# First FFN of a two-block transformer kernel: high and low activations side by side in the up projection, and the gate's row steps in the down stage

## The chip, the cores and the metric

The kernel runs on one core of a Trainium2 chip. The metric is the device time of one execution in microseconds; the time before is the median of three runs, 758.73 us (757.24 to 759.23).

## The reference, cut to what matters

Two transformer blocks on one sequence of 256 rows of width 1024, in fp32. The change touches only the feed-forward part of the first block and the gate `g2`, which is a row vector of 1024:

```python
c_act = jax.nn.silu(c)
mod = c_act @ w_ada[l] + b_ada[l]
sh1, sc1, g1, sh2, sc2, g2 = [m[:, None, :] for m in jnp.split(mod, 6, axis=-1)]
...
h = rmsnorm(x, norm_gains[l, 2]) * (1.0 + sc2) + sh2
y = jnp.square(jax.nn.relu(h @ w1[l] + b1[l])) @ w2[l] + b2[l]
x = x + g2 * rmsnorm(y, norm_gains[l, 3])
```

`w1` is 1024 x 4096, `w2` 4096 x 1024. The second block has a mixer of four branches and a second FFN (SwiGLU, hidden width 2816).

## The kernel before, in words

**Split products.** Every large product is made of three products of fp32r parts: high weight x high activation, high x low, low x high. Weights come in units of 128 x 1024 values (512 KB). Each unit goes through four engines: SyncE (queue SP) loads it into one of four slots of `raw`; ScalarE (ACT) rounds it to its high part `wh` (`round_unit`, L614); VectorE (DVE) subtracts that from `raw` to get the low part `wl` (`low_unit`, L1000); TensorE (PE) multiplies. The rings `raw`, `wh`, `wl` have four slots each. ACT may round unit u when PE has finished unit u - 4 (semaphore `unit_done`), DVE follows (`rounded`), PE starts unit u when DVE is through (`split_ready`), and SP loads unit u + 4 once DVE is through with unit u. ACT and DVE run `AHEAD` = 3 units ahead of PE: while PE is on unit u, they prepare unit u + 3. The order of each engine's work is written out by hand, and every wait is on the engine that stands in the list: what comes behind it waits too.

**Up stage of the first FFN (units `U_UP1` to `U_UP1` + 31).** A loop of eight turns with four units in each (`RING` = 4). Unit k gives 128 hidden columns for all 256 rows, in PSUM bank `acc[k % 4]`. The transposed activations `xT` hold the high parts in columns 0 to 255 and the low parts in 256 to 511. PE does `col_unit` (L1445 to L1447): for each of 8 k-tiles three matmuls of 256 columns, all into the same 256 columns of the bank. For each unit, ACT rounds the weights of unit k + 3, makes relu with bias out of the bank (L803, which frees the bank), and squares it into the high part of `hid` (L805). DVE makes the low weights of unit k + 3 (L1000), the exact square (L1202) and the low part of `hid` (L1205).

**The gate's rows.** `g2` is summed as rows: for each of 8 row blocks of `w_ada` (128 x 1024, 512 KB) ACT's queue issues a load into `xr[:, 0, :]` (`rows_tmp`, L808), and DVE adds block x c to `G2` (L1210, 128 x 1024). There is one buffer: a load waits for the step before it (`g2_used`), a step waits for its load (`g2_full`). In the kernel before, one such load and one such step stand in each of the eight turns of the up loop. After the eighth, GpSimd multiplies `G2` by the gain (L570). PE sums it over the partitions after 28 of the 32 down units.

**Down stage (units `U_DOWN1` to `U_DOWN1` + 31).** `wide_unit`: 12 matmuls of 512 columns for a unit, into all four banks (L1466 to L1468). Beside it ACT only rounds (`round_down1`) and DVE only makes low weights (`low_down1`), except for the bias `b2`: behind its first turn of four units ACT clears and rounds `b2parts` (L823, L824, three times L811); behind the third and the fifth turn it rounds two rows and one row more. DVE subtracts for it behind its second turn (two instructions of L1214) and behind its fourth (one).

**The second FFN's up stage** runs much later (570 to 697 us) and uses `both_unit` (L1458, L1459): for each k-tile one matmul of 512 columns (high weight x high and low activations side by side) and one of 256 (low weight x high). ACT copies the right half of the bank (L978), DVE adds the left half to it (L1412).

Of the kernel before, what the change touches and what calls it, by code (L numbers as in the profile page):

```python
# [50 lines left out]
RING = 4  # L51
# [15 lines left out]
V_B1, V_CONV, V_GQ, V_GK, V_BSP, V_ROWS = 16, 48, 54, 55, 56, 60  # L67
# [110 lines left out]
def build_program(nc, a):  # L178
# [25 lines left out]
    with ctx:  # L204
# [3 lines left out]
        def sem(name):  # L208
            return ctx.enter_context(nc.semaphore(name))
# [142 lines left out]
        arg_psum, w_exped, w_masked, pvs_done, sb_ready, fox_ready = (sem(n) for n in ("arg_psum", "w_exped", "w_masked", "pvs_done", "sb_ready", "fox_ready"))  # L352
        dve_step, pool_step = sem("dve_step"), sem("pool_step")
        out_ready, out_done = sem("out_ready"), sem("out_done")
        b2_zeroed, b2_high, b2_rest = sem("b2_zeroed"), sem("b2_high"), sem("b2_rest")
        f_parts = sem("f_parts")
        wf_zeroed = sem("wf_zeroed")
# [3 lines left out]
        def slot_of(u):  # L361
            return u % RING
# [243 lines left out]
        def _(act):  # L606
# [15 lines left out]
            def round_looped(u0, i, k):  # L622

                s, count = raw_place(u0 + k)
                round_unit(raw_full[s], raw_slot(s), 16 * count + 16 * i, u0 + k - RING + 1 + RING * i, s)
# [169 lines left out]
                high_columns(X_UP1, r)  # L795
            round_static(U_UP1 + 2)

            with act.Fori(0, D_FF // P // RING) as i:
                for k in range(RING):
                    round_looped(U_UP1 + AHEAD, i, k)  # L800
                    act.wait_ge(unit_done, U_UP1 + k + 1 + RING * i)
                    act.wait_ge(hid_ready, RING * i + k + 1)
                    A(act_t[:, k, :], acc[k][:, 0:ROWS], ACT.Relu, bias=vT[:, bass.ds(V_B1 + k + RING * i, 1)]).then_inc(acc_free, 1)  # L803
                    act.wait_ge(acc_free, F_PROJ1 + k + 1 + RING * i)
                    A(hid[:, RING * i + k, 0:ROWS], act_t[:, k, :], ACT.Square).then_inc(hid_hi, 1)  # L805
                    if k == 1:
                        act.wait_ge(g2_used, i + 1)
                        act.dma_start(xr[:, 0, :], w_ada_rows[bass.ds(P * i, P), D * C_G2:]).then_inc(g2_full, 16)  # L808
            def b2_round(row):

                A(b2parts[row:row + 1, :], b2row[row:row + 1, :], ACT.Copy).then_inc(b2_high, 1)  # L811

            def round_down1(first, count):

                with act.Fori(0, count) as i:
                    for k in range(RING):
                        round_looped(U_DOWN1 + AHEAD + RING * first, i, k)

            round_down1(0, 1)
            act.wait_ge(late_loaded, 16 * 8)  # L820
            act.wait_ge(unit_done, U_DOWN1)
            for half in range(2):
# [2 lines left out]
            act.wait_ge(b2_zeroed, 2)  # L825
            for row in (0, 32, 64):
                b2_round(row)
            round_down1(1, 2)
            act.wait_ge(b2_rest, 2)
            for row in (32, 64):  # L830
                b2_round(row)
            round_down1(3, 2)
            act.wait_ge(b2_rest, 3)
            b2_round(64)
            round_down1(5, D_FF // P // RING - 6)
# [151 lines left out]
        def _(dve):  # L987
# [207 lines left out]
            low_static(U_UP1 + 1)  # L1195
            low_static(U_UP1 + 2)

            with dve.Fori(0, D_FF // P // RING) as i:
                for k in range(RING):
                    low_unit(U_UP1 + AHEAD + k + 1 + RING * i, slot_of(U_UP1 + AHEAD + k), slot_of(U_UP1 + AHEAD + k))  # L1200
                    dve.wait_ge(acc_free, F_PROJ1 + k + 1 + RING * i)
                    V.tensor_tensor(val_t[:, k, :], act_t[:, k, :], act_t[:, k, :], ALU.mult).then_inc(hid_sq, 1)  # L1202
                    dve.wait_ge(hid_sq, RING * i + k + 1)
                    dve.wait_ge(hid_hi, RING * i + k + 1)
                    V.tensor_tensor(hid[:, RING * i + k, ROWS:], val_t[:, k, :], hid[:, RING * i + k, 0:ROWS].bitcast(f32),  # L1205
                                    ALU.subtract).then_inc(hid_ready, 1)

                dve.wait_ge(g2_full, 16 * i + 32)
                dve.wait_ge(g2_used, i + 1)
                V.scalar_tensor_tensor(out=G2[:, :], in0=xr[:, 0, :], scalar=cT[:, bass.ds(i, 1)], in1=G2[:, :],  # L1210
                                       op0=ALU.mult, op1=ALU.add).then_inc(g2_used, 1)
            def b2_remainder(row):

                V.tensor_tensor(b2row[row:row + 1, :], b2row[row:row + 1, :], b2parts[row:row + 1, :].bitcast(f32), ALU.subtract).then_inc(b2_rest, 1)  # L1214

            def low_down1(first, count):

                with dve.Fori(0, count) as i:
                    for k in range(RING):
                        u = U_DOWN1 + AHEAD + RING * first + k  # L1220
                        low_unit(u + 1 + RING * i, slot_of(u), slot_of(u))

            low_down1(0, 2)
            dve.wait_ge(b2_high, 3)
            for row in (32, 64):
                b2_remainder(row)
            low_down1(2, 2)
            dve.wait_ge(b2_high, 5)
            b2_remainder(64)
            low_down1(4, D_FF // P // RING - 5)  # L1230
# [199 lines left out]
        def _(pe):  # L1430
# [5 lines left out]
            def col_unit(u, wait, bank, moving, waits=None):  # L1436

                s = slot_of(u)
                pe.wait_ge(split_ready, wait)
                for kt in range(KT):  # L1440
                    if waits is not None:
                        pe.wait_ge(xT_ready, waits(kt))
                    w = slice(P * kt, P * (kt + 1))
                    hi, lo = moving[:, kt, 0:ROWS], moving[:, kt, ROWS:]
                    mm(bank[:, 0:ROWS], wh[:, s, w], hi, start=(kt == 0), stop=False)  # L1445
                    mm(bank[:, 0:ROWS], wh[:, s, w], lo, start=False, stop=False)  # L1446
                    ins = mm(bank[:, 0:ROWS], wl[:, s, w], hi, start=False, stop=(kt == KT - 1))  # L1447
                ins.then_inc(unit_done, 1)

            def both_unit(u, wait, bank, moving, waits=None):  # L1450

                s = slot_of(u)
                pe.wait_ge(split_ready, wait)
                for kt in range(KT):
                    if waits is not None:
                        pe.wait_ge(xT_ready, waits(kt))
                    w = slice(P * kt, P * (kt + 1))
                    mm(bank[:, :], wh[:, s, w], moving[:, kt, :], start=(kt == 0), stop=False, skip_group_check=True)  # L1458
                    ins = mm(bank[:, 0:ROWS], wl[:, s, w], moving[:, kt, 0:ROWS], start=False, stop=(kt == KT - 1),  # L1459
                             skip_group_check=True)  # L1460
                ins.then_inc(unit_done, 1)
# [83 lines left out]
            def columns_ready(t):  # L1545

                return lambda kt: X_COUNT * t + KT + 2 * (kt // 2) + 2
# [169 lines left out]
            with pe.Fori(0, D_FF // P // RING) as i:  # L1717
                for k in range(RING):
                    pe.wait_ge(acc_free, F_PROJ1 - RING + k + 1 + RING * i)
                    col_unit(U_UP1 + k, U_UP1 + k + 1 + RING * i, acc[k], xT, columns_ready(X_UP1) if k == 0 else None)  # L1720
            n_hid = D_FF // P
            for k in range(n_hid - RING):
                pe.wait_ge(hid_ready, RING + k + 1)
# [222 lines left out]
```

## Time and profile before

| | |
|---|---|
| median of three runs | 758.73 us (757.24 to 759.23) |
| the profiled execution | 759.55 us |
| its span, first to last instruction | 757.8 us |
| PE busy (matmul) | 722.2 us, 95% |
| PE weight loads | 615.5 us, 81% |
| DVE busy | 513.7 us, 68% |
| ACT busy | 444.4 us, 59% |
| GpSimd busy | 37.8 us, 5% |
| DMA | 152.07 MB, mean 201 GB/s |
| granted TensorE clock | 1.000 |

The profile is of one execution. Matmuls are pipelined, so the duration of one (some 0.28 us for 256 columns) is longer than the distance to the next, and only the distances tell the pace. An instruction of DVE can start a little before the end shown for the one in front of it. A wait is shown in brackets behind the instruction that waited, with what released it.

### The profile page before, as it was taken

The numbers are of one execution on the slowest core, as the hardware profiler recorded it, in microseconds if no ns is written. First come the engines' busy times: TensorE is split into PE (matmuls) and PEld (weight loads), VectorE is DVE, ScalarE is ACT, GpSimd is POOL, SyncE is SP. The second block draws the span as 40 slices with busy tenths as digits, with TensorE's granted clock in tenths as the row PEclk, the third lists the DMA queues.
The fourth block names the chain that finished last, engine by engine and source line by source line (L and its number), as shares of the span: only waits on it lengthen the run. The fifth ranks groups of instructions, "written<-read, shape, count | busy, mean of one in ns | idle before, by whom it ended". The sixth has DMA issues, their size and how long they took to land.

```text
span 757.8 us, 12098 instructions
## 1 busy us (share of the span) xinstructions
PE 722.2 (95%) x4126; PEld 615.5 (81%) x4126; DVE 513.7 (68%) x738; ACT 444.4 (59%) x696; POOL 37.8 (5%) x69
## 2 busy tenths in 40 slices
PE   0599999999999999999999999999999999999998
PEld 0488976689999888877989787787788888888886
DVE  6788579788777765447647574856677777777443
ACT  0554768656666654455546497465457777776331
POOL 4000000100000100014102000000000000000000
PEclk9999999999999999999999999999999999999999
DMA  8999778447877766545764654555445665665651
GB/s 309 364 331 378 209 221 301 139 141 220 243 222 255 246 197 195 194 112 136 224 189 146 223 147 134 191 163 180 130 139 167 187 198 171 188 196 194 194 194 56
DMA packets 137554, 152.07 MB, mean 201 GB/s; under 512 B 6189, under 2 KB 111784, under 8 KB 137516
## 3 DMA queue, kind: packets, MB, share of 16 engines
q1 hardware_dynamic: 135714, 146.86, 62.6%
q10 hardware_dynamic: 1804, 4.74, 1.8%
q8 instruction: 22, 0.36, 0.2%
q14 instruction: 14, 0.11, 0.0%
HBM read 150.14 MB, written 1.44 MB: 200 GB/s over the span
## 4 chain that ended last, share of the span: by engine, by line
PE 52%; DVE 2%; issue 0%; ACT 0%; DVEq 0%; ACTq 0%
PE acc L1458 11%; PE acc L1466 10%; PE acc L1467 9%; PE acc L1468 9%; PE acc L1459 6%; PE acc L1447 1%; PE acc L1445 1%; PE acc L1446 1%; PE aux L1434 1%; DVE wl L1000 0%; DVE x_rows L1069 0%; PE aux L1660 0%; ACT wh L614 0%; PE aux L1778 0%; PE aux L1852 0%
## 5 line engine op out<-in xcount | busy, mean ns | idle before, releaser
L1000 DVE TENSOR_TENSOR wl<-raw,wh 128x1024 fp32r<-128x1024 f32 x215 | 263.6, 1232 | 147.0 <-ACT wh L614 146.0
L614 ACT ACTIVATE wh<-raw 128x1024 fp32r<-128x1024 f32 x215 | 226.0, 1056 | 122.4 <-PE acc L1468 116.1
L1445 PE MATMUL acc<-xT,wh 128*128 128x256 f32 x440 | 125.2, 285 | 3.4 <-DVE xT L1042 2.2
L1458 PE MATMUL acc<-xT,wh 128*128 128x512 f32 x352 | 124.5, 399 | 0.3 <-DVE xT L1033 0.3
L1446 PE MATMUL acc<-xT,wh 128*128 128x256 f32 x440 | 124.5, 283 | 0.0
L1447 PE MATMUL acc<-xT,wl 128*128 128x256 f32 x440 | 124.5, 283 | 0.0
L1466 PE MATMUL acc<-wh,xT 128*128 128x512 f32 (+1 forms) x272 | 108.0, 397 | 0.3 <-issue 0.3
L1467 PE MATMUL acc<-wl,xT 128*128 128x512 f32 (+1 forms) x272 | 104.3, 384 | 0.0
L1468 PE MATMUL acc<-wh,xT 128*128 128x512 f32 (+1 forms) x272 | 104.3, 383 | 0.0
L1459 PE MATMUL acc<-xT,wl 128*128 128x256 f32 x352 | 98.9, 281 | 0.0
L1445 PEld LDWEIGHTS acc<-xT,wh 128*128 128x128 f32 x440 | 84.4, 192 | 5.8 <-DVE xT L1042 2.3
L1446 PEld LDWEIGHTS acc<-xT,wh 128*128 128x128 f32 x440 | 84.4, 192 | 0.1
L1447 PEld LDWEIGHTS acc<-xT,wl 128*128 128x128 f32 x440 | 84.4, 192 | 0.0
L1466 PE MATMUL acc<-wh,hid 128*128 128x512 f32 x216 | 84.1, 390 | 0.0
L1467 PE MATMUL acc<-wl,hid 128*128 128x512 f32 x216 | 84.1, 389 | 0.0
L1468 PE MATMUL acc<-wh,hid 128*128 128x512 f32 x216 | 84.0, 389 | 0.0
L1458 PEld LDWEIGHTS acc<-xT,wh 128*128 128x128 f32 x352 | 66.1, 188 | 17.1 <-issue 0.7
L1459 PEld LDWEIGHTS acc<-xT,wl 128*128 128x128 f32 x352 | 66.5, 189 | 0.0
L1466 PEld LDWEIGHTS acc<-wh,xT 128*128 128x128 f32 x272 | 51.1, 188 | 16.2 <-issue 6.6
L1468 PEld LDWEIGHTS acc<-wh,xT 128*128 128x128 f32 x272 | 51.1, 188 | 10.4
L1467 PEld LDWEIGHTS acc<-wl,xT 128*128 128x128 f32 x272 | 51.2, 188 | 9.3 <-issue 0.5
L1466 PEld LDWEIGHTS acc<-wh,hid 128*128 128x128 f32 x216 | 40.6, 188 | 8.4
(278 smaller groups left out, 864.4 us busy)
## 6 DMA issues: line engine op xcount, KB each, us to landing
raw<-in_w_in SPq DMA_DIRECT2D x66, 512.0 KB, 4.1
raw<-in_w SPq DMA_DIRECT2D x64, 512.0 KB, 4.3
raw<-in_w_ffn_in SPq DMA_DIRECT2D x44, 512.0 KB, 4.4
raw<-in_w_ada SPq DMA_DIRECT2D x29, 512.0 KB, 5.9
raw<-in_w_ffn_out SPq DMA_DIRECT2D x22, 512.0 KB, 4.2
raw_more<-in_w_ada SPq DMA_DIRECT2D x11, 512.0 KB, 6.7
raw<-in_w_out SPq DMA_DIRECT2D x11, 512.0 KB, 3.3
rows_tmp<-in_w_ada ACTq DMA_DIRECT2D x8, 512.0 KB
```

The costliest lines, as they stand in the source:

```text
L614: A(wh[:, s, :], raw_unit, ACT.Copy).then_inc(rounded, 1)
L1000: V.tensor_tensor(wl[:, s, :], raw_slot(r), wh[:, s, :].bitcast(f32), ALU.subtract).then_inc(split_ready, 1)
L1434: return mm(out, in_, ident[0:n, 0:n], start=True, stop=True, is_transpose=True)
L1445: mm(bank[:, 0:ROWS], wh[:, s, w], hi, start=(kt == 0), stop=False)
L1446: mm(bank[:, 0:ROWS], wh[:, s, w], lo, start=False, stop=False)
L1447: ins = mm(bank[:, 0:ROWS], wl[:, s, w], hi, start=False, stop=(kt == KT - 1))
L1458: mm(bank[:, :], wh[:, s, w], moving[:, kt, :], start=(kt == 0), stop=False, skip_group_check=True)
L1459: ins = mm(bank[:, 0:ROWS], wl[:, s, w], moving[:, kt, 0:ROWS], start=False, stop=(kt == KT - 1), skip_group_check=True)
L1466: mm(bank, hi, wh[:, s, cols], start=first, stop=False)
L1467: mm(bank, hi, wl[:, s, cols], start=False, stop=False)
L1468: return mm(bank, lo, wh[:, s, cols], start=False, stop=last)
```

## The change

- PE: the up units of the first FFN use `both_unit` instead of `col_unit`. The high activations' product and the low activations' product with the high weights stand side by side in the 512 columns of the bank.
- ACT, up stage: instead of relu with bias, it copies the right half of the bank with the bias added (`up_half`). The high part of `hid` is now a copy of DVE's exact square (`hidden_high`), one unit behind (for the fourth unit of a turn at once).
- DVE, up stage: it adds the left half (`acc_free` comes from here now), makes max(x, 0) * x in one instruction, and makes the low part of `hid` one unit behind (`hidden_low`). The row step is taken out.
- The eight loads and eight row steps of `g2` stand in the down stage: one load ahead of it, the others behind the second and the fourth unit of each turn on ACT, and the steps behind the first and the third unit of each turn on DVE, for the first four turns.
- ACT's wait on `hid_ready` ahead of the relu falls away.

```diff
@@ ACT, up stage
+            def hidden_high(i, k):
+                act.wait_ge(hid_sq, RING * i + k + 1)
+                A(hid[:, RING * i + k, 0:ROWS], val_t[:, k, :], ACT.Copy).then_inc(hid_hi, 1)
+
             with act.Fori(0, D_FF // P // RING) as i:
                 for k in range(RING):
                     round_looped(U_UP1 + AHEAD, i, k)
                     act.wait_ge(unit_done, U_UP1 + k + 1 + RING * i)
-                    act.wait_ge(hid_ready, RING * i + k + 1)
-                    A(act_t[:, k, :], acc[k][:, 0:ROWS], ACT.Relu, bias=vT[:, bass.ds(V_B1 + k + RING * i, 1)]).then_inc(acc_free, 1)
-                    act.wait_ge(acc_free, F_PROJ1 + k + 1 + RING * i)
-                    A(hid[:, RING * i + k, 0:ROWS], act_t[:, k, :], ACT.Square).then_inc(hid_hi, 1)
-                    if k == 1:
-                        act.wait_ge(g2_used, i + 1)
-                        act.dma_start(xr[:, 0, :], w_ada_rows[bass.ds(P * i, P), D * C_G2:]).then_inc(g2_full, 16)
+                    A(act_t[:, k, :], acc[k][:, ROWS:], ACT.Identity, bias=vT[:, bass.ds(V_B1 + k + RING * i, 1)]).then_inc(up_half, 1)
+                    if k >= 1:
+                        hidden_high(i, k - 1)
+                    if k == RING - 1:
+                        hidden_high(i, k)
@@ ACT, down stage
+            def load_gate_rows(first, i):
+                act.wait_ge(g2_used, i + 1 + first)
+                act.dma_start(xr[:, 0, :], w_ada_rows[bass.ds(P * i + P * first, P), D * C_G2:]).then_inc(g2_full, 16)
+
-            def round_down1(first, count):
+            def round_down1(first, count, loads=()):
                 with act.Fori(0, count) as i:
                     for k in range(RING):
                         round_looped(U_DOWN1 + AHEAD + RING * first, i, k)
-            round_down1(0, 1)
+                        if k in loads:
+                            load_gate_rows(2 * first + (k + 1) // 2, 2 * i)
+
+            act.wait_ge(g2_used, 1)
+            act.dma_start(xr[:, 0, :], w_ada_rows[0:P, D * C_G2:]).then_inc(g2_full, 16)
+            round_down1(0, 1, (1, 3))
...
-            round_down1(1, 2)
+            round_down1(1, 2, (1, 3))
...
-            round_down1(3, 2)
+            round_down1(3, 1, (1,))
+            round_down1(4, 1)
@@ DVE, up stage
+            def hidden_low(i, k):
+                dve.wait_ge(hid_hi, RING * i + k + 1)
+                V.tensor_tensor(hid[:, RING * i + k, ROWS:], val_t[:, k, :], hid[:, RING * i + k, 0:ROWS].bitcast(f32),
+                                ALU.subtract).then_inc(hid_ready, 1)
+
             with dve.Fori(0, D_FF // P // RING) as i:
                 for k in range(RING):
                     low_unit(U_UP1 + AHEAD + k + 1 + RING * i, slot_of(U_UP1 + AHEAD + k), slot_of(U_UP1 + AHEAD + k))
+                    dve.wait_ge(up_half, RING * i + k + 1)
+                    V.tensor_tensor(act_t[:, k, :], acc[k][:, 0:ROWS], act_t[:, k, :], ALU.add).then_inc(acc_free, 1)
+                    if k >= 1:
+                        hidden_low(i, k - 1)
                     dve.wait_ge(acc_free, F_PROJ1 + k + 1 + RING * i)
-                    V.tensor_tensor(val_t[:, k, :], act_t[:, k, :], act_t[:, k, :], ALU.mult).then_inc(hid_sq, 1)
-                    dve.wait_ge(hid_sq, RING * i + k + 1)
-                    dve.wait_ge(hid_hi, RING * i + k + 1)
-                    V.tensor_tensor(hid[:, RING * i + k, ROWS:], val_t[:, k, :], hid[:, RING * i + k, 0:ROWS].bitcast(f32),
-                                    ALU.subtract).then_inc(hid_ready, 1)
-
-                dve.wait_ge(g2_full, 16 * i + 32)
-                dve.wait_ge(g2_used, i + 1)
-                V.scalar_tensor_tensor(out=G2[:, :], in0=xr[:, 0, :], scalar=cT[:, bass.ds(i, 1)], in1=G2[:, :],
+                    V.scalar_tensor_tensor(out=val_t[:, k, :], in0=act_t[:, k, :], scalar=0.0, in1=act_t[:, k, :],
+                                           op0=ALU.max, op1=ALU.mult).then_inc(hid_sq, 1)
+                hidden_low(i, RING - 1)
@@ DVE, down stage
+            def gate_rows(first, i):
+                dve.wait_ge(g2_full, 16 * i + 32 + 16 * first)
+                dve.wait_ge(g2_used, i + 1 + first)
+                V.scalar_tensor_tensor(out=G2[:, :], in0=xr[:, 0, :], scalar=cT[:, bass.ds(i + first, 1)], in1=G2[:, :],
                                        op0=ALU.mult, op1=ALU.add).then_inc(g2_used, 1)
-            def low_down1(first, count):
+            def low_down1(first, count, steps_of_two=False):
                 with dve.Fori(0, count) as i:
                     for k in range(RING):
                         u = U_DOWN1 + AHEAD + RING * first + k
                         low_unit(u + 1 + RING * i, slot_of(u), slot_of(u))
-            low_down1(0, 2)
+                        if steps_of_two and k % 2 == 0:
+                            gate_rows(2 * first + k // 2, 2 * i)
+            low_down1(0, 2, True)
...
-            low_down1(2, 2)
+            low_down1(2, 2, True)
@@ PE, up stage
-                    col_unit(U_UP1 + k, U_UP1 + k + 1 + RING * i, acc[k], xT, columns_ready(X_UP1) if k == 0 else None)
+                    both_unit(U_UP1 + k, U_UP1 + k + 1 + RING * i, acc[k], xT, columns_ready(X_UP1) if k == 0 else None)
```

## Rows read from the trace of the kernel before

**Rows 1.** Page, part 1: busy time of PE over the span.

```profile
PE 722.2 (95%) x4126; PEld 615.5 (81%) x4126; DVE 513.7 (68%) x738; ACT 444.4 (59%) x696; POOL 37.8 (5%) x69
```

**Rows 2.** Windows: busy time of PE, PEld, DVE, ACT, POOL; clock, DMA share, GB/s.

```profile
163.00:251.00 88.00, 88.00 (x734) 87.96 (x733) 69.23 (x99) 57.62 (x92) 0.00 (x0) 1.00 0.80 247
...
252.00:328.00 76.00, 76.00 (x336) 62.87 (x335) 41.45 (x33) 37.94 (x38) 3.31 (x1) 1.00 0.63 198
...
55.00:75.00 20.00, 19.68 (x118) 17.10 (x118) 17.45 (x17) 8.97 (x13) 0.00 (x0) 1.00 1.06 381
...
260.00:262.00 2.00, 2.00 (x11) 1.65 (x10) 1.23 (x1) 2.00 (x5) 0.00 (x0) 1.00 1.03 283
```

**Rows 3.** Instructions of one line: ns min/median/max, first and last start in us.

```profile
L803 ACT ACTIVATE act_t<-acc,vT x32: 474/474/478, 161.7 to 251.0; 128x256 f32<-128x256 f32 x32
...
L1458 PE MATMUL acc<-xT,wh x352: 395/398/472, 570.2 to 694.3; 128*128 128x512 f32 x176
```

**Rows 4.** Timeline of DVE in the up stage: start, duration (us), instruction.

```profile
196.17 1.22 DVE L1000 TENSOR_TENSOR wl<-raw,wh 128x1024 fp32r<-128x1024 f32 x1
197.30 0.42 DVE L1202 TENSOR_TENSOR val_t<-act_t 128x256 f32<-128x256 f32 x1
197.90 0.43 DVE L1205 TENSOR_TENSOR hid<-val_t,hid 128x256 f32 x1 [0.18 <-DVE val_t L1202]
198.25 1.23 DVE L1000 TENSOR_TENSOR wl<-raw,wh 128x1024 fp32r<-128x1024 f32 x1
```

**Rows 5.** Groups by line and form: busy us, mean ns of one, idle before.

```profile
L1412 DVE TENSOR_TENSOR val_t<-acc,act_t 128x256 f32<-128x256 f32 x44 | 18.5, 421 | 3.4 <-ACT act_t L978 3.4
...
L1210 DVE SCALAR_TENSOR_TENSOR G<-rows_tmp,cT,G 128x1024 f32<-128x1024 f32 x8 | 10.2, 1281 | 1.6 <-DMA rows_tmp<-in_w_ada 1.6
...
L811 ACT ACTIVATE xT<-b2row 1x1024 fp32r<-1x1024 f32 x6 | 6.3, 1057 | 0.1
```

**Rows 6.** Timeline of PE and ACT where the down stage begins.

```profile
250.59 0.40 PE L1466 MATMUL acc<-wh,hid 128*128 128x512 f32 x1
...
251.57 0.42 ACT L805 ACTIVATE hid<-act_t 128x256 f32 x1
...
259.04 1.06 ACT L614 ACTIVATE wh<-raw 128x1024 fp32r<-128x1024 f32 x1 [1.66 <-PE acc L1468]
260.00 1.14 ACT L823 ACTIVATE xT<-ones 65x512 fp32r<-65x512 f32 x2
...
264.48 2.01 ACT L614 ACTIVATE wh<-raw 128x1024 fp32r<-128x1024 f32 x2
```

**Rows 7.** Timeline of DVE in the down stage.

```profile
265.57 2.36 DVE L1000 TENSOR_TENSOR wl<-raw,wh 128x1024 fp32r<-128x1024 f32 x2 [4.21 <-ACT wh L614]
...
272.21 2.46 DVE L1214 TENSOR_TENSOR b2row<-b2row,xT 1x1024 f32<-1x1024 f32 x2
...
298.15 1.23 DVE L1000 TENSOR_TENSOR wl<-raw,wh 128x1024 fp32r<-128x1024 f32 x1 [1.49 <-ACT wh L614]
300.87 1.23 DVE L1000 TENSOR_TENSOR wl<-raw,wh 128x1024 fp32r<-128x1024 f32 x1 [1.49 <-ACT wh L614]
```

**Rows 8.** Row loads (issue, use, ACT queue's packets in 250.0 to 250.5); landing of L463.

```profile
234.53 0.34 ACTq L808 DMA_DIRECT2D rows_tmp<-in_w_ada  x1
...
242.72 1.29 DVE L1210 SCALAR_TENSOR_TENSOR G<-rows_tmp,cT,G 128x1024 f32<-128x1024 f32 x1 [1.58 <-DMA rows_tmp<-in_w_ada]
...
246.04 0.34 ACTq L808 DMA_DIRECT2D rows_tmp<-in_w_ada  x1
...
q10 hardware_dynamic: 1, 0.00, 0.1%
...
DMA to landing us min/median/max: 3.3/4.3/8.3
```

**Rows 9.** One line each: DVE's low weights from 254.5 to 256, GpSimd's product.

```profile
L1000 DVE TENSOR_TENSOR wl<-raw,wh x2: 1222/2326/3429, 253.8 to 254.9; 128x1024 fp32r<-128x1024 f32 x2
...
L570 POOL TENSOR_TENSOR G<-G,rows_tmp x1: 3315/3315/3315, 253.9 to 253.9; 128x1024 f32<-128x1024 f32 x1
```

More of the change, by code:

```diff
@@ L354, in build_program @@
         out_ready, out_done = sem("out_ready"), sem("out_done")
+        up_half = sem("up_half")
         b2_zeroed, b2_high, b2_rest = sem("b2_zeroed"), sem("b2_high"), sem("b2_rest")
@@ L1200, in _ @@
                     low_unit(U_UP1 + AHEAD + k + 1 + RING * i, slot_of(U_UP1 + AHEAD + k), slot_of(U_UP1 + AHEAD + k))
+                    dve.wait_ge(up_half, RING * i + k + 1)
+                    V.tensor_tensor(act_t[:, k, :], acc[k][:, 0:ROWS], act_t[:, k, :], ALU.add).then_inc(acc_free, 1)
+                    if k >= 1:
+                        hidden_low(i, k - 1)
                     dve.wait_ge(acc_free, F_PROJ1 + k + 1 + RING * i)
-                    V.tensor_tensor(val_t[:, k, :], act_t[:, k, :], act_t[:, k, :], ALU.mult).then_inc(hid_sq, 1)
-                    dve.wait_ge(hid_sq, RING * i + k + 1)
-                    dve.wait_ge(hid_hi, RING * i + k + 1)
-                    V.tensor_tensor(hid[:, RING * i + k, ROWS:], val_t[:, k, :], hid[:, RING * i + k, 0:ROWS].bitcast(f32),
-                                    ALU.subtract).then_inc(hid_ready, 1)
-                dve.wait_ge(g2_full, 16 * i + 32)
-                dve.wait_ge(g2_used, i + 1)
-                V.scalar_tensor_tensor(out=G2[:, :], in0=xr[:, 0, :], scalar=cT[:, bass.ds(i, 1)], in1=G2[:, :],
-                                       op0=ALU.mult, op1=ALU.add).then_inc(g2_used, 1)
+                    V.scalar_tensor_tensor(out=val_t[:, k, :], in0=act_t[:, k, :], scalar=0.0, in1=act_t[:, k, :],
+                                           op0=ALU.max, op1=ALU.mult).then_inc(hid_sq, 1)
+                hidden_low(i, RING - 1)
             def b2_remainder(row):
                 V.tensor_tensor(b2row[row:row + 1, :], b2row[row:row + 1, :], b2parts[row:row + 1, :].bitcast(f32), ALU.subtract).then_inc(b2_rest, 1)
-            def low_down1(first, count):
+            def gate_rows(first, i):
+                dve.wait_ge(g2_full, 16 * i + 32 + 16 * first)
+                dve.wait_ge(g2_used, i + 1 + first)
+                V.scalar_tensor_tensor(out=G2[:, :], in0=xr[:, 0, :], scalar=cT[:, bass.ds(i + first, 1)], in1=G2[:, :],
+                                       op0=ALU.mult, op1=ALU.add).then_inc(g2_used, 1)
+            def low_down1(first, count, steps_of_two=False):
                 with dve.Fori(0, count) as i:
```

## The prediction

> **What bounds the kernel now.** First the busy shares: PE is busy for 95% of the span [rows 1]. Then the stages. In the up stage (163 to 251 us) and in the down stage (252 to 328 us) PE is busy all the time at clock 1.00; DVE and ACT are busy for 79% and 65% in the first, 55% and 50% in the second, and the DMA engines for 80% and 63% [rows 2]. So PE sets the pace in both. A change gains only by what it takes from PE, and loses when a weight tile comes late.
>
> How much cover is there? A unit's rounding on ACT may start when PE has finished the unit four before it; its remainder on DVE follows, and PE wants it three units after that start. I count from PE's first down matmul (t = 0, 250.59) [rows 6]. DVE's remainders in the down stage follow each other by 2.72 us [rows 7], which is PE's time for a unit: PE wants down unit k at t = 2.72 k.
>
> **Part 1, the up matmuls.** Before, a unit is 24 matmuls of 256 columns; afterwards 8 of 512 and 8 of 256: the same number of columns, but 16 weight loads in place of 24. The bank evictions of the old form run from 161.7 to 251.0 for 32 units: 89.3/31 = 2.881 us a unit. The second FFN already has the new form: 352 pairs from 570.2 to 694.3, 124.1/351 = 0.3536 us a pair, 2.829 us a unit [rows 3]. Saved: (2.881 - 2.829) x 32 = **1.7 us**. The bounds are 0 (PE counts columns only) and 1.7; both rows are of this kernel, so I take 1.7.
> The Trainium skill, "TensorE: Matmul & The Clock Gate", section "Back-to-back issue gap", gives an isolated gap of N/2.4 + 2.5 ns; by that the saving would be 8 x 2.5 ns a unit, 0.6 us in all, and the old unit would take 2.62 us. The trace has 2.88, so it does not agree.
>
> **Part 2, DVE and ACT in the up stage.** ACT keeps three instructions a unit (rounding 1.06, eviction 0.47, a copy in place of the square 0.42) [rows 6, 3]: nothing. DVE gets an addition from PSUM, 0.42 each [rows 5], and loses the row step, 1.28 once in four units. DVE instructions that do not wait overlap a little: a small subtraction holds it for 0.35, a weight remainder for 1.13, and one that needs DVE's last result starts 0.60 after it [rows 4]. Four units: 4 x 1.13 for the weight remainders, 12 x 0.35 for the small ones, 0.25 once for the addition with nothing between it and its reader (k = 0), 0.7 for the trip to ACT and back at k = 3, and 0.75 while ACT then makes the next rounding: 10.4 us, against PE's 11.3. The cover is 0.9 us in four units, and behind it the three units of weights. Cost: nothing. Only the last unit has a longer tail: eviction, addition, another subtraction, square, then the copy, so ACT is through at about t = 2.3 rather than 1.0. The first down unit wants its last bank at t = 2.0, and the addition frees it at 1.4: hidden.
>
> **Part 3, the row steps in the down stage.** This is where the time goes. Eight loads of 512 KB and eight steps of 1.28 us [rows 5] move from one in four units to one in two, with one buffer. The chain is: DVE finishes step n, ACT issues load n+1, it lands, DVE does step n+1. ACT waits for step n ahead of its next roundings, and DVE waits for the landing ahead of its next remainders. A turn costs L + 1.28 + 0.25 (from release to issue, an estimate), where L runs from issue to DVE's start. PE takes 5.44 for two units, so every L above 3.9 loses ground, and also takes up cover that the ACT work on b2 needs.
>
> What is L? The trace shows it once as a wait, 234.53 to 242.72 = 8.2 us, in a stretch with loads of two more rows beside it; the load of 246.04, beside down weights, has its last packet between 250.0 and 250.5, so at least 4.0. Down weights of the same size land in 3.3 at best and 4.3 in the median [rows 8]. Bounds: 3.3 and 8.2. I take **4.6**, the median and 0.3 for the hand-over to DVE, because those loads run beside each other as the new ones will.
>
> With L = 4.6:
> - Load 0 leaves at t = 2.5, step 0 ends at 8.4. Load 1 leaves at 8.6, step 1 ends at 14.5. Unit 6 is ready at 15.7 (wanted 16.3).
> - Load 2 leaves at 14.8, and only then does ACT come to the block that clears and rounds b2. That block is 264.48 - 260.00 = 4.5 us and stands now at t = 9.4 [rows 6]; unit 7 is now ready at 265.57 + 1.2, t = 16.2, of wanted 19.0 [rows 7]. It moves to 15.3, so unit 7 is ready at 22.1: **3.1 us late**.
> - Step 2 ends at 23.3, step 3 at 29.4, unit 10 ready at 30.6: 0.3 more. DVE's b2 remainders (2.46 for two) [rows 7] are then no longer in its idle time: 0.9 more.
> - Steps 4 and 5, turns of 6.13 against 5.44, less the slack then there: 0.5 more.
> - ACT rounds two b2 rows (1.06 each) [rows 5] between load 6 and unit 15: 1.4 more. Step 7: 0.3 more.
> - GpSimd's product of G2 (3.3 us) starts when step 7 is done. Now it stretches one DVE remainder to 3.43 instead of 1.22 [rows 9], under cover; then there is none, and a b2 remainder stands there too: 1.9 more.
> Sum: **8.4 us** of PE waiting in front of down units 7 to 19. After step 7 the old slack comes back, but lost time of PE isn't won back, as PE is the bound from there to the end.
>
> **The sum.** 8.4 - 1.7 = +6.7 us. The profiled execution took 759.55 (span 757.8), 0.8 above the median of 758.73. From the profiled one it is 766.3, from the median **765.4**. The same list with L = 4.0 gives 5.2 of waiting (+3.5, 762.2), with L = 5.3 13.0 (+11.3, 770.0).
>
> **The rivals.**
> *Loads land as lone ones do (not slower).* Place: ACT's load 2 ahead of the b2 block. If rows land in L = 3.3 to 3.7, the list gives 1.7 to 3.7 of waiting, less 1.7: 0 to +2.0, about 759.7. It decides at L = 3.8. If the block had cover left altogether, 757.0. For it: the best landings of 3.3, and that waiting PE asks for fewer weights, so the DMA engines grow emptier. Against: the load of 246.04, over 4.0. Chance 0.22.
> The Trainium skill, "DMA: Bandwidth & Descriptors", section "Anatomy of one DMA — SWDGE (gpsimd) path", fits a transfer as 2.0 us + bytes/436e3: 3.2 us for 512 KB, an estimate for this load; the list would give 759 by it. The trace's 3.3 at best agrees, its 4.3 in the median doesn't.
> *The DMA engines are the bound.* Three loads of 0.524 MB in 5.44 us are 289 GB/s. The weights of the down stage alone go at 198, with a share of 0.63; two bunched ones had a share of 1.03 at 283 GB/s. Against: 381 GB/s from 55 to 75 us [rows 2]. Then L is 5.7, waiting 15.8: +14.1, 772.8. Chance 0.10.
> *The hand-overs in the up stage are longer than I count.* Above 0.9 us more in four units, DVE falls behind PE; at 1.25 more it is 8 x 0.35 = 2.8 us behind at the stage's end, which puts load 0 and all that hangs on it off by as much: about 768. Chance 0.06.
> *The wide matmuls bring nothing* here: 767.1; it lies in the forecast's own range.
>
> **The numbers.** Forecast 0.62 (762.2 to 770.0), rivals 0.22, 0.10, 0.06. The range goes from 757.0, the not-slower case without waiting, to 770. It leaves out the DMA-bound case and little else. A measurement can tell about 0.3%, 2.3 us, from no change. Faster by that needs more than the whole of part 1: 0.04. Within it: nearly all of the not-slower case, 0.20. Slower: 0.76.
>
> **What would show it.** In the up stage: wide pairs at 0.353 us, a unit at 2.83, PE never waiting. In the down stage: PE waiting for DVE's remainders at units 7, 10, 11, 14, 15, 18 and 19, some 8 us; DVE waiting for row loads; the b2 block on ACT starting at t = 15 instead of 9.4; the DVE step on G2 once in 6.1 us. Wrong would be: PE busy throughout from unit 3 to 20 (then the first rival), L above 5.5 with a DMA share near 1 (the second), idle PE in the up stage (the third), or a wait anywhere behind unit 20.

## The result, and the profile after

The changed kernel takes **763.83 us**, the median of 6 runs (762.47 to 764.59), against 758.71 us (756.63 to 759.38) for the kernel before, measured beside it: ratio **1.0079**, 95% interval 1.0064 to 1.0094. That is 6.0 us by the ratio (0.0079 x 758.7), 5.1 by the medians. It is slower. The forecast was +6.7 us (765.4). One of the 8 runs of e6 below took 2533.65 us, and its ratio leaves that run out.

Busy time and the waits of PE. First the page's part 1 and two of the groups in part 5 (busy us, mean ns of one, idle before):

```profile
PE 720.4 (95%) x3870; PEld 602.2 (79%) x3870; DVE 524.2 (69%) x770; ACT 439.0 (58%) x696; POOL 37.7 (5%) x69
...
L1014 DVE TENSOR_TENSOR wl<-raw,wh 128x1024 fp32r<-128x1024 f32 x215 | 261.2, 1221 | 134.5 <-ACT wh L615 133.2
...
L1486 PE MATMUL acc<-xT,wh 128*128 128x512 f32 x608 | 211.0, 392 | 1.1 <-DVE xT L1047 1.1
```

PE has 256 matmuls and 1.8 us of busy time less than [rows 1], and still 95%: the share shows neither the gain nor the waits, so the stages have to be looked at one by one. The windows of the two stages, the same as in [rows 2], then the down stage in five pieces (columns: window, its length, busy PE, PEld, DVE, ACT, POOL with counts; clock, DMA share, GB/s):

```profile
163.00:251.00 88.00, 88.00 (x506) 76.80 (x505) 73.67 (x127) 55.03 (x95) 0.00 (x0) 1.00 0.71 210
252.00:328.00 76.00, 69.96 (x302) 55.87 (x301) 46.62 (x37) 34.15 (x36) 3.33 (x1) 1.00 0.70 229
...
262.00:274.00 12.00, 10.54 (x47) 8.44 (x46) 5.54 (x5) 8.43 (x10) 0.00 (x0) 1.00 0.60 193
274.00:286.00 12.00, 10.08 (x44) 7.73 (x43) 9.13 (x8) 3.83 (x4) 0.00 (x0) 1.00 0.70 236
286.00:298.00 12.00, 10.94 (x47) 8.48 (x46) 6.89 (x7) 5.82 (x7) 0.00 (x0) 1.00 0.77 253
298.00:310.00 12.00, 10.40 (x45) 8.03 (x44) 9.93 (x7) 5.68 (x6) 3.33 (x1) 1.00 0.55 191
310.00:322.00 12.00, 12.00 (x55) 9.94 (x54) 6.14 (x6) 4.37 (x5) 0.00 (x0) 1.00 0.84 276
```

PE never waits in the up stage. In the down stage, full before, it is idle 6 us; from 310 on it is full again. The DMA engines are busier (0.70 against 0.63), far from 1, and the clock is 1.00 in all these windows: neither is the bound.

Up stage, instructions of one line (ns min/median/max, first and last start). ACT's eviction, once a unit, answers to L803 of [rows 3], the wide matmul to L1458:

```profile
L808 ACT ACTIVATE act_t<-acc,vT x32: 455/476/478, 162.8 to 248.8; 128x256 f32<-128x256 f32 x32
...
L1486 PE MATMUL acc<-xT,wh x256: 392/395/467, 159.7 to 248.1; 128*128 128x512 f32 x128
```

A unit takes (248.8 - 162.8)/31 = 2.774 us, against 2.881. Next the timeline of PE in the down stage, the starts of some units with PE's wait in brackets; and the view of PE's waits from 245 to 335 us (total, times, longest):

```profile
269.17 0.47 PE L1494 MATMUL acc<-wh,hid 128*128 128x512 f32 x1 [1.46 <-DVE wl L1014]
...
278.73 0.47 PE L1494 MATMUL acc<-wh,hid 128*128 128x512 f32 x1 [1.14 <-DVE wl L1014]
282.48 0.47 PE L1494 MATMUL acc<-wh,hid 128*128 128x512 f32 x1 [0.78 <-DVE wl L1014]
294.96 0.47 PE L1494 MATMUL acc<-wh,hid 128*128 128x512 f32 x1 [1.06 <-DVE wl L1014]
...
307.99 0.47 PE L1494 MATMUL acc<-wh,hid 128*128 128x512 f32 x1 [1.60 <-DVE wl L1014]
```
```profile
PE acc L1494 <- DVE wl L1014: 6.0, 5, 1.6
```

The bracket counts from the modelled end of the last matmul. What PE loses is the distance between two starts less the usual 0.227 us (308.52 to 308.75, say); the distance to the next start, 0.31 instead of 0.227, is counted with it. At unit 7 the last start before the wait is 267.32: 1.85 - 0.23 + 0.08 = 1.7. So read, and the units counted from the first down matmul at 248.48, units 7, 10, 11, 14, 15, 18 and 19 lose 1.7, 1.4, 1.0, 0.2, 1.3, 0.2 and 1.8: **7.7 us** (the sum is of the unrounded values; the last 0.2 of the stage's 7.9, below, is in gaps too small to list). The expectation of e2 below has it as 7.5.

**Where the time went**, in the two profiled executions (763.25 and 759.55 us, +3.7). The up matmuls begin 1.28 us later, in code that the change leaves alone; from there to the first down matmul 88.82 us against 92.21 (-3.4); from first to last down matmul of the first FFN 97.83 against 89.94 (+7.9); and the second FFN's up stage, the same code in both, takes 2.3 us less in the profile after. The first and the last are differences between two executions (more of this under e7); in the one after, the granted clock was 0.50 from 31.2 to 34.6 and from 41.4 to 44.8 us, where the one before had 1.00, which may be the 1.28. The change itself is the middle two, and the -3.4 has part of the same luck in it.

The chain that sets the waits, on ACT (the rounding of weights L615, issues of row loads L831 and L820, the b2 block L836 to L815):

```profile
250.78 0.36 ACTq L831 DMA_DIRECT2D rows_tmp<-in_w_ada  x1
...
256.29 0.36 ACTq L820 DMA_DIRECT2D rows_tmp<-in_w_ada  x1
256.75 2.01 ACT L615 ACTIVATE wh<-raw 128x1024 fp32r<-128x1024 f32 x2 [3.43 <-DVE G L1239]
261.66 0.33 ACTq L820 DMA_DIRECT2D rows_tmp<-in_w_ada  x1
262.22 1.16 ACT L836 ACTIVATE xT<-ones 65x512 fp32r<-65x512 f32 x2 [3.46 <-DVE G L1239]
...
266.71 2.00 ACT L615 ACTIVATE wh<-raw 128x1024 fp32r<-128x1024 f32 x2
270.42 0.35 ACTq L820 DMA_DIRECT2D rows_tmp<-in_w_ada  x1
```

And on DVE (row steps L1239, remainders of weights L1014, of b2 L1233):

```profile
254.98 1.28 DVE L1239 SCALAR_TENSOR_TENSOR G<-rows_tmp,cT,G 128x1024 f32<-128x1024 f32 x1 [1.35 <-DMA rows_tmp<-in_w_ada]
...
260.34 1.28 DVE L1239 SCALAR_TENSOR_TENSOR G<-rows_tmp,cT,G 128x1024 f32<-128x1024 f32 x1 [1.27 <-DMA rows_tmp<-in_w_ada]
...
267.80 1.23 DVE L1014 TENSOR_TENSOR wl<-raw,wh 128x1024 fp32r<-128x1024 f32 x1 [5.04 <-ACT wh L615]
...
276.16 1.28 DVE L1239 SCALAR_TENSOR_TENSOR G<-rows_tmp,cT,G 128x1024 f32<-128x1024 f32 x1 [2.94 <-DMA rows_tmp<-in_w_ada]
...
303.27 3.31 DVE L1233 TENSOR_TENSOR b2row<-b2row,xT 1x1024 f32<-1x1024 f32 x1
```

Read both together. ACT issues load 1 at 256.29, as soon as step 0 is through (254.98 + 1.28); the load is used at 260.34; step 1 ends at 261.62 and ACT, idle since 258.76, issues load 2 at 261.66. Only then comes the b2 block, at 262.22 (the 3.46 in its bracket) against 260.00 in [rows 6] though the stage began 2.1 us earlier; the rounding behind it starts at 266.71, so DVE's remainder for unit 7 starts at 267.80 after 5.04 us without work, and PE waits until 269.17.

### The profile page after: what moved, and what is told of

Its sections match the earlier page's. It is cut to its first block, busy times and chain, and to the rows that moved or that the text cites. A ratio compares the mean times of both kernels' runs of the same rounds, so it can differ in the third digit from the quotient of the medians.

```text
span 761.5 us, 11571 instructions
## 1 busy us (share of the span) xinstructions
PE 720.4 (95%) x3870; PEld 602.2 (79%) x3870; DVE 524.2 (69%) x770; ACT 439.0 (58%) x696; POOL 37.7 (5%) x69
## 4 chain that ended last, share of the span: by engine, by line
PE 50%; DVE 2%; ACT 1%; issue 1%; DVEq 0%; ACTq 0%
PE acc L1486 11%; PE acc L1494 9%; PE acc L1496 9%; PE acc L1495 9%; PE acc L1487 6%; PE acc L1475 1%; PE acc L1473 1%; PE acc L1474 1%; PE aux L1462 1%; DVE wl L1014 0%; DVE x_rows L1083 0%; PE aux L1688 0%; ACT wh L615 0%; PE aux L1806 0%; PE aux L1880 0%
## 5 line engine op out<-in xcount | busy, mean ns | idle before, releaser
L1014 DVE TENSOR_TENSOR wl<-raw,wh 128x1024 fp32r<-128x1024 f32 x215 | 261.2, 1221 | 134.5 <-ACT wh L615 133.2
L615 ACT ACTIVATE wh<-raw 128x1024 fp32r<-128x1024 f32 x215 | 225.2, 1055 | 119.5 <-PE acc L1496 90.8
L1486 PE MATMUL acc<-xT,wh 128*128 128x512 f32 x608 | 211.0, 392 | 1.1 <-DVE xT L1047 1.1
L1486 PEld LDWEIGHTS acc<-xT,wh 128*128 128x128 f32 x608 | 113.8, 187 | 27.1 <-issue 1.6
L1487 PEld LDWEIGHTS acc<-xT,wl 128*128 128x128 f32 x608 | 114.6, 188 | 0.0
L1496 PEld LDWEIGHTS acc<-wh,xT 128*128 128x128 f32 x272 | 51.1, 188 | 10.4
L1473 PE MATMUL acc<-xT,wh 128*128 128x256 f32 x184 | 53.5, 291 | 2.0 <-DVE xT L1056 1.6
L1494 PEld LDWEIGHTS acc<-wh,hid 128*128 128x128 f32 x216 | 40.5, 188 | 17.0 <-issue 8.8
L1474 PE MATMUL acc<-xT,wh 128*128 128x256 f32 x184 | 52.8, 287 | 0.0
L1496 PEld LDWEIGHTS acc<-wh,hid 128*128 128x128 f32 x216 | 40.5, 188 | 8.5
L1495 PEld LDWEIGHTS acc<-wl,hid 128*128 128x128 f32 x216 | 40.6, 188 | 8.1
L1107 DVE SCALAR_TENSOR_TENSOR ada_sum<-raw,cT,ada_sum 128x1024 f32<-128x1024 f32 x29 | 37.2, 1282 | 5.3 <-DMA raw<-in_w_ada 4.0
```

What stands on the lines that cost most here:

```text
L615: A(wh[:, s, :], raw_unit, ACT.Copy).then_inc(rounded, 1)
L1107: V.scalar_tensor_tensor(out=sums, in0=raw_slot(place % FIRST_RING), scalar=cT[:, kt:kt + 1], in1=sums, op0=ALU.mult, op1=ALU.add).then_in ...
L1494: mm(bank, hi, wh[:, s, cols], start=first, stop=False)
L1495: mm(bank, hi, wl[:, s, cols], start=False, stop=False)
L1496: return mm(bank, lo, wh[:, s, cols], start=False, stop=last)
```

## The experiments

Each is the changed kernel with the edit shown. The first four were timed beside each other (the kernel before: 757.17 us), the next three in a second set (757.29 us); the last is a single run. In all of them the time that PE loses in the down stage is read as above.

**e1_wide_up_only**: part 1 and 2 alone; the row loads and steps go back to one in four units of the up stage.

```diff
@@ ACT, up stage, in the loop over k
+                    if k == 1:
+                        act.wait_ge(g2_used, i + 1)
+                        act.dma_start(xr[:, 0, :], w_ada_rows[bass.ds(P * i, P), D * C_G2:]).then_inc(g2_full, 16)
@@ DVE, up stage, behind hidden_low(i, RING - 1)
+                dve.wait_ge(g2_full, 16 * i + 32)
+                dve.wait_ge(g2_used, i + 1)
+                V.scalar_tensor_tensor(out=G2[:, :], in0=xr[:, 0, :], scalar=cT[:, bass.ds(i, 1)], in1=G2[:, :],
+                                       op0=ALU.mult, op1=ALU.add).then_inc(g2_used, 1)
@@ down stage: no row loads on ACT, no row steps on DVE
```

> The up stage of the changed kernel, with the row loads and row steps back where they were before (one in each turn of the up loop), and the down stage of before. Theory (the loss is the row steps in the down stage): the changed profile has a unit every 2.774 us against 2.881, 3.4 us less for the stage, so 755.3 (3.4 below the kernel before), PE without a wait in the down stage. DVE has then 10.4 + 1.2 = 11.6 us of work in a turn in which PE takes 11.1, so it falls back by 0.5 us a turn, 4 us in all, which the three units of weights in hand cover. Rival (the hand-overs between ACT and DVE are what costs): DVE's turn is longer than 11.9 us, PE waits in the up stage, and the kernel is no faster than before or slower.

Measured: 755.85 us, median of 12, ratio **0.9979** (0.9964 to 0.9995): faster than the changed kernel and, narrowly, than the one before. PE waits neither in the up stage nor in the down stage, whose matmuls take 89.94 us from first to last, to the hundredth what they took before. The window of the up stage, and the wide matmuls there:

```profile
160.00:250.00 90.00, 90.00 (x509) 77.90 (x508) 80.98 (x135) 56.69 (x94) 0.00 (x0) 1.00 0.79 250
```
```profile
L1490 PE MATMUL acc<-xT,wh x256: 395/398/468, 157.6 to 247.8; 128*128 128x512 f32 x128
```

DVE carries the row steps beside the new additions at 90% busy, and its turn of four units is 11.31 us, PE's own, not the 11.6 expected. In e7, the same kernel, PE's turn is 11.1 us (32 pairs at 0.347), and there too PE never waits in this stage. There was room for the steps without the move.

**e2_rows_down_only**: the other half. The up stage in the narrow form of before without its row steps, the down stage as changed.

```diff
@@ ACT, up stage
-                    A(act_t[:, k, :], acc[k][:, ROWS:], ACT.Identity, bias=vT[:, bass.ds(V_B1 + k + RING * i, 1)]).then_inc(up_half, 1)
+                    A(act_t[:, k, :], acc[k][:, 0:ROWS], ACT.Relu, bias=vT[:, bass.ds(V_B1 + k + RING * i, 1)]).then_inc(acc_free, 1)
...
@@ PE, up stage
-                    both_unit(U_UP1 + k, U_UP1 + k + 1 + RING * i, acc[k], xT, columns_ready(X_UP1) if k == 0 else None)
+                    col_unit(U_UP1 + k, U_UP1 + k + 1 + RING * i, acc[k], xT, columns_ready(X_UP1) if k == 0 else None)
```

> The up stage of before (three matmuls of 256 columns), without its row loads and steps, and the down stage of the changed kernel. Theory: the waits of PE at down units 7 to 19 stay, 7.5 us in the changed profile, so +7.5, 766.2. Rival (the waits come from the later end of the new up stage's last unit on ACT): ACT reaches the first row load at t = 1.2 instead of 2.3, and the waits shrink by two thirds or more: below 762.

Measured: 767.2 us, median of 6, ratio **1.0121** (1.0094 to 1.0148). PE's waits from 245 to 335 us:

```profile
PE acc L1479 <- DVE wl L1008: 7.5, 7, 1.6
```

By starts it loses 9.2 us, at the same seven units (table below). So the whole loss, and nothing of the gain, goes with the moved rows.

**e3_two_buffers**: all of the change, but with a second buffer for the rows, each load issued one step earlier.

```diff
+            def row_buffer(n):
+                return xr[:, 0, :] if n % 2 == 0 else tmpT[:, :, :].rearrange("p t n -> p (t n)")
...
-                act.wait_ge(g2_used, i + 1 + first)
-                act.dma_start(xr[:, 0, :], w_ada_rows[bass.ds(P * i + P * first, P), D * C_G2:]).then_inc(g2_full, 16)
+                act.wait_ge(g2_used, i + first)
+                act.dma_start(row_buffer(first), w_ada_rows[bass.ds(P * i + P * first, P), D * C_G2:]).then_inc((g2_full, g2_full2)[first % 2], 16)
```

> The changed kernel with a second row buffer (a tile that is free after the first projection): load n+1 leaves when step n-1 is done, so that it is under way during step n and neither ACT nor DVE waits for it. Theory (the turn of one load and one step through one buffer is the cause): the waits at units 7, 10, 14, 15, 18 go, what is left is DVE's own work around its b2 remainders and GpSimd's product, at most 2 us; 758.7 - 3.4 + 0 to 2 = 755.3 to 757.3. Rival (three loads in two units are too much for the DMA engines): row loads then take 8 us or more, PE still waits for 5 us or more, above 760.

Measured: 756.76 us, median of 12, ratio **0.998** (0.9965 to 0.9994). The same eight loads and eight steps in the same places, and of seven waits one small one is left, at unit 7 (0.9 us by starts). It is not the one expected to stay, which was DVE's own work around the b2 remainders and the product: ACT's b2 block starts at 264.00, still behind a wait for step 1, which ends at 263.40. PE's waits from 245 to 335, and the window of the down stage:

```profile
PE acc L1502 <- DVE wl L1018: 0.6, 1, 0.6
```
```profile
252.00:320.00 68.00, 67.37 (x297) 55.49 (x296) 46.59 (x40) 34.12 (x36) 3.32 (x1) 1.00 0.76 257
```

The DMA engines move more here in a microsecond than in the changed kernel (257 GB/s against 232 in the same window) while PE is at work for 67.4 of 68 us: they aren't the bound. The buffer's turn is.

**e5_one_load**: all eight steps, but seven of the eight row loads left out (the steps take the first block's rows again, so G2 is not the reference's).

```diff
             def load_gate_rows(first, i):
-                act.wait_ge(g2_used, i + 1 + first)
-                act.dma_start(xr[:, 0, :], w_ada_rows[bass.ds(P * i + P * first, P), D * C_G2:]).then_inc(g2_full, 16)
+                return
...
-                dve.wait_ge(g2_full, 16 * i + 32 + 16 * first)
+                dve.wait_ge(g2_full, 32)
```

> The changed kernel with only the first of the eight row loads; all eight steps on DVE are made, from the same rows (so G2 is not the gate: seven loads are left out). Theory (waits for the landings): the waits of PE fall to those that DVE's and GpSimd's own work makes, under 2 us; 755.3 to 757. If instead the steps' own 1.28 us on DVE, or the shared path with GpSimd, were the cause, 5 us or more of waiting would stay: 761 or more.

Measured: 755.74 us, median of 10, ratio **0.9977** (0.9962 to 0.9991); PE waits nowhere in the down stage. The steps' own 1.28 us each cost nothing on DVE. Only with the loads' turn in front of them do they.

**e6_block_first**: ACT makes the b2 block ahead of its wait for load 2.

```diff
-            round_down1(0, 1, (1, 3))
+            round_down1(0, 1, (1,))
...
             for row in (0, 32, 64):
                 b2_round(row)
+            load_gate_rows(2, 0)
```

> The changed kernel, with ACT's b2 block (4.5 us) ahead of its wait for row load 2 instead of behind it. Theory (the block came late because it stood behind the wait for step 1): the block starts at t = 11 instead of 13.7, unit 7 is ready at t = 18.2, and PE's 1.7 us in front of it go; load 2 leaves at t = 15.6 instead of 13.2, so that unit 8 is ready at 22.4 against 21.8, 0.6 late; the other waits stay: 763.8 - 1.1 = 762.7. Rival (unit 7 is late because DVE's own work or the weight load is late): the wait at unit 7 stays as it is.

Measured: 762.33 us, median of 8, ratio **1.0052** (1.0034 to 1.007), against 762.7 expected. The wait at unit 7 is gone, and so is the one at unit 10, which was not expected: load 3 is issued at 268.24 instead of 270.42 and takes 5.0 us instead of 5.7. ACT's timeline shows why unit 7 is in time: the block begins at 259.25, behind a rounding and no longer behind DVE's step.

```profile
259.25 1.14 ACT L836 ACTIVATE xT<-ones 65x512 fp32r<-65x512 f32 x2
```

**e4_product_later**: GpSimd's product of G2 waits until DVE is through with the weight remainder of the down stage's unit 23, so that it no longer runs beside DVE's last b2 remainder.

```diff
             pool.wait_ge(g2_used, KT + 1)
+            pool.wait_ge(split_ready, U_DOWN1 + 24)
```

> The changed kernel, with GpSimd's product of G2 held back until DVE is through with down unit 20's neighbourhood (a wait on the weight remainder of unit 23). Theory: in the changed profile PE waits 1.8 us in front of unit 19, because one of DVE's instructions in the shadow of the product takes 2.1 us more; with the product later, where DVE is ahead again, that wait goes and the others stay: 763.8 - 1.8 = 762.0. Rival (the b2 remainder alone, 1.2 us on DVE, makes that wait): it stays above 1 us, and the time does not change.

Measured: 763.07 us, median of 10, ratio 1.0068 (1.005 to 1.0086): the point is 1 us above the 762.0 expected, and its interval overlaps the changed kernel's. The timeline has the effect looked for. The b2 remainder takes 1.22 us in place of 3.31, the product alone 2.39 in place of 3.33, and the wait at unit 19 (1.8) is gone:

```profile
304.33 1.22 DVE L1234 TENSOR_TENSOR b2row<-b2row,xT 1x1024 f32<-1x1024 f32 x1
```
```profile
313.53 2.39 POOL L572 TENSOR_TENSOR G<-G,rows_tmp 128x1024 f32<-128x1024 f32 x1 [160.04 <-DVE wl L1015]
```

In this execution something else took its place. PE lost 2.1 us at unit 14 instead of 0.2: the row load ahead of it was issued at 282.92 and used at 289.40, 6.5 us where the changed kernel's took 4.6.

```profile
289.40 1.28 DVE L1240 SCALAR_TENSOR_TENSOR G<-rows_tmp,cT,G 128x1024 f32<-128x1024 f32 x1 [3.69 <-DMA rows_tmp<-in_w_ada]
```

Soon after that wait the granted clock fell for a few microseconds (windows on either side and of the stretch itself):

```profile
286.00:293.00 7.00, 5.15 (x24) 3.96 (x23) 2.42 (x2) 1.59 (x2) 0.00 (x0) 1.00 0.62 197
293.00:297.00 4.00, 4.00 (x12) 2.88 (x11) 2.36 (x3) 2.53 (x3) 0.00 (x0) 0.57 0.54 212
297.00:304.00 7.00, 7.00 (x33) 5.77 (x32) 4.54 (x5) 3.66 (x4) 0.00 (x0) 1.00 0.87 298
```

A matmul there comes 0.43 us after the last instead of 0.227: the level of 1.2 GHz, 1.7 us lost by starts. Most of that replaces the wait at unit 15, whose remainder ended only at 295.86: at the full clock PE would have come to it at 294.76 (292.27 + 11 x 0.227, an estimate) and have waited there. So the local effect is shown by the timeline; that it is worth 1.8 us of the whole is not: 1.0079 less 1.0068 is 0.8 us, with intervals of over 1 us on each.

**e8_loads_on_gpsimd_queue**: one buffer still, but GpSimd's queue issues the row loads, so ACT never waits for a step.

```diff
@@ GpSimd, ahead of the product
+            pool.wait_ge(hid_hi, D_FF // P)
+            for n in range(KT):
+                pool.wait_ge(g2_used, n + 1)
+                pool.dma_start(xr[:, 0, :], w_ada_rows[P * n:P * (n + 1), D * C_G2:]).then_inc(g2_rows, 16)
@@ ACT: the eight waits and issues go
```

> The changed kernel, with the eight row loads issued from GpSimd's queue, one buffer as before. ACT waits for no step and issues no load; DVE still waits for each landing. This parts the two waits. If ACT's wait for the step were the larger part, PE's waits fall to under 3 us: 759 or less. Theory (the turn of load and step through one buffer paces DVE, whoever issues): the wait at unit 7 goes (1.7 us), those at 10, 11, 14, 18 and 19 stay or grow with the landing from this queue; 5 to 8 us of waiting, 761 to 765.

Measured: 764.5 us, median of 4, ratio **1.0087** (1.0063 to 1.0112), no better than the changed kernel. The wait at unit 7 is gone, as the b2 block is free again. But the turn is as long as before, and DVE waits for the landing in front of its remainders, so PE loses 7.2 us at units 6, 8, 10, 11, 14, 16, 18 and 19. The issue of load 1, on GpSimd, and the step that uses it, on DVE:

```profile
257.77 0.54 POOL L573 DMA_DIRECT2D rows_tmp<-in_w_ada  x1 [5.64 <-DVE G L1241]
```
```profile
262.55 1.28 DVE L1241 SCALAR_TENSOR_TENSOR G<-rows_tmp,cT,G 128x1024 f32<-128x1024 f32 x1 [2.82 <-DMA rows_tmp<-in_w_ada]
```

From issue to use 4.8 us, from step to step (256.18 to 262.55) 6.4. It isn't who stands in the wait that counts, but that one buffer is loaded and used in turn.

**e7_wide_up_only_again**: the kernel of e1 once more, one run with its profile, for the pace of the wide matmuls.

> The kernel of e1 once more, for its pace. In its first profile a pair of matmuls took 0.3537 us in the first FFN's up stage and 0.347 in the second's; in the changed kernel's both took 0.347, in the one with a single row load 0.347 and 0.354, in the kernel before 0.354 in the second. If the pace belongs to the code's place, this profile has 0.3537 and 0.347 again; if it belongs to the execution, one of them differs.

Measured: 754.53 us. The same line of the same code:

```profile
L1490 PE MATMUL acc<-xT,wh x256: 392/395/467, 159.1 to 247.5; 128*128 128x512 f32 x128
```

That is 88.4/255 = 0.347 us a pair, where e1's profile has 0.3537, both at clock 1.00. The pace belongs to the execution, not to the code's place or neighbours.

Time lost by PE in front of each down unit (us, from one profiled execution each; "1.2 GHz" is the stretch at that clock; sums are of unrounded values). The last column is the down stage's time from the first to the last matmul, less the 89.94 of before; it takes in what is too small to list:

| kernel | 7 | 10 | 11 | 14 | 15 | 18 | 19 | others | sum | stage |
|---|---|---|---|---|---|---|---|---|---|---|
| forecast | 3.1 | 0.3 | 0.9 | 0.5 | 1.4 | 0.3 | 1.9 | | 8.4 | |
| changed | 1.7 | 1.4 | 1.0 | 0.2 | 1.3 | 0.2 | 1.8 | | 7.7 | 7.9 |
| e2 | 1.7 | 1.4 | 1.0 | 0.7 | 1.3 | 1.2 | 1.8 | | 9.2 | 9.4 |
| e8 | 0 | 0.5 | 1.0 | 1.1 | 0 | 0.5 | 1.8 | 2.2 | 7.2 | 7.5 |
| e4 | 1.9 | 0.7 | 1.0 | 2.1 | 0 | 0 | 0 | 1.7 at 1.2 GHz | 7.3 | 7.5 |
| e6 | 0 | 0 | 0.8 | 0.6 | 1.3 | 0.4 | 1.8 | | 5.0 | 5.1 |
| e3 | 0.9 | 0 | 0 | 0 | 0 | 0 | 0 | | 0.9 | 0.9 |
| e1, e5 | 0 | 0 | 0 | 0 | 0 | 0 | 0 | | 0 | 0.0 |

## Why the prediction was right

**Part 1, 1.7 us: right in kind, the size depends on the execution.** The wide pair was taken at 0.3536 us from [rows 3]. Five profiles have 0.3537 in the first FFN (e1, e3, e4, e6, e8) and three have 0.347 (changed, e5, and e7, which is e1's kernel); by the second pace the saving is 3.4 us, above the 1.7 that the prediction took as its upper bound. Over many executions e1, which is this part with part 2, gives 0.0021 x 757.2 = 1.6 us (0.4 to 2.7). The lower bound of the term (0) and the rival "wide matmuls bring nothing" are out, narrowly: its interval ends at 0.9995. The Trainium skill's gap in "TensorE: Matmul & The Clock Gate", section "Back-to-back issue gap", an isolated one, gave an estimate of 0.6 us. The interval of e1 holds that too; but by the same gap a pair would take 0.325 us, and no profile here has less than 0.347.

**Part 2, cost nothing: right, and with more room than was used.** PE is busy all through the up stage. The estimate of a 10.4 us turn on DVE against 11.3 was made without the row step; e1 puts the step (1.28) back and still PE doesn't wait, though DVE is 90% busy. The rival "hand-overs are longer" is out. That room is what the change gave away: the move of the rows was not needed to pay for the addition.

**Part 3, 8.4 us of waiting: right in mechanism and places, 7.7 in size.** PE waits at the seven units named, at nothing behind 19. e3 and e5 show that the turn of load and step through one buffer is the cause: a second buffer leaves 0.9 us, no loads leave nothing. e8 shows that it is the turn and not ACT's standing in it. The sizes of its terms were off, one against the other:
- L was taken as 4.6. The first two loads have 4.20 (250.78 to 254.98) and 4.05 (256.29 to 260.34), the next one that DVE waited for 5.74 (270.42 to 276.16), the other two 4.63 and 4.77. The mean of the five is 4.7. The 0.25 from release to issue was too much: 0.03 to 0.20 (261.62 to 261.66, 283.53 to 283.72). The steps were to come once in 6.1 us; they come 5.4 to 8.6 us apart, the last four 6.1 to 6.4.
- Because the first two were quick, the b2 block came at t = 13.7, not 15.3, and unit 7 was 1.7 us late, not 3.1. The 5.74 then made unit 10 late by 1.4, not 0.3. That these two nearly cancel is luck.
- The b2 remainders' 0.9, the rounding's 1.4 and GpSimd's 1.9 are 1.0, 1.3 and 1.8. The last was [rows 9] moved to a place without cover, and e4 shows the wait at 19 go with the product. Unit 7's term was the b2 block behind load 2, and e6 shows it go with that order.

The Trainium skill, "DMA: Bandwidth & Descriptors", section "Anatomy of one DMA — SWDGE (gpsimd) path", has a fit that gives an estimate of 3.2 us for 512 KB. That was the rival "loads land as lone ones do" (759.7). The loads that DVE waited for took 4.05 to 5.74 from issue to use on ACT's queue in the changed kernel (6.5 once in e4), and 4.4 to 5.3 on GpSimd's in e8, beside the weights: the measurement decides against it. For the rival "DMA engines are the bound" one load came to 5.74, and the stage's mean share of 0.70 hides what the engines did meanwhile. The stretches of load 1 (4.05) and of load 3 (5.74):

```profile
256.30:260.30 4.00, 4.00 (x20) 3.30 (x19) 2.33 (x2) 2.01 (x2) 0.00 (x0) 1.00 0.73 204
270.40:276.20 5.80, 5.80 (x27) 4.83 (x26) 2.22 (x3) 2.01 (x2) 0.00 (x0) 1.00 0.89 305
```

So the long load had more traffic beside it. But the load of 4.63 had a share of 0.90 too, so what makes one long is open. As the bound of the stage they are out: e3 moved more in less time, and PE hardly waited.

**The sum.** 7.7 to 7.9 of waiting less 1.6 by e1 is +6.1 to +6.3; +6.0 is measured, +6.7 was forecast. The excess is the part of the 8.4 us that part 3 was too large by. The parts alone don't quite add up: e1 and e2 give -1.6 and +9.2 (0.0121 x 757.2), together +7.6 (+4.4 to +10.8 with the bounds added) against +6.0 (+4.9 to +7.1). The intervals overlap; the loads of e2 took up to 5.8 us more often (5.1, 4.3, 5.8, 5.1, 5.8), and why is open.

## What to carry to other kernels

Work that is moved from a stage where it comes once in four units to one where it comes once in two has to be priced as a turn: landing, use and release of its buffer, against the time that the bound engine takes between two. Here that is 4.7 + 1.28 + 0.03 to 0.20 = 6.0 to 6.2 us against 5.44, and a second buffer removes nearly all of it, while busy shares of 55% say nothing of it. And before work is moved to make room, try the change without the move: the engine at 90% still kept up, and that version (0.9979) is level with the one of two buffers (0.998); of those that make all eight loads none was faster.

## What the runs showed that was not expected

- **Two paces of the same matmuls.** A pair of one 512-column and one 256-column matmul comes every 0.347 or every 0.3537 us, by execution, and also by stage within one: e1's profile has 0.3537 in the first FFN and 0.347 in the second, e5's the reverse, both at clock 1.00 with PE never idle. For the 352 pairs of the second FFN that is 2.3 us, more than the 1.6 that e1 gained. What sets it is open.
- **An instruction held up by another engine.** DVE's b2 remainder, 1.22 us in e4, takes 3.31 beside GpSimd's product, and the product 3.33 beside DVE, 2.39 alone. The product is recorded from 302.18 to 305.51, the remainder from 303.27 to 306.58, which is 1.07 us after the product's end, not far from its own 1.22. The Trainium skill, "SBUF — State Buffer", section "Who interferes with whom", says that a DVE instruction with two inputs in SBUF contends with a GpSimd instruction that reads SBUF, and that what they share is an exclusive lock. The trace agrees: the remainder stood until the product was through. The product's own 0.94 more fits it as well: DVE's weight remainder of 302.02 to 303.24 was there first, and 305.51 - 2.39 is 303.12.
- **The clock after a wait.** In e4's profile PE lost 2.1 us at unit 14, and the granted clock was 0.57 from 293 to 297. No such stretch follows the waits of up to 1.8 us in the changed kernel's down stage, whose windows all have 1.00, nor e4's own wait of 1.9 at unit 7. Whether the wait brought it is not shown.
